# One pair of score products for both key streams of the first query tile, in a two-layer attention trunk

## The reference

```python
qr = rope(q, cos, sin)
o_slc = causal_attention(qr, rope(k_s), v_s)      # stream 0
o_win = causal_attention(qr, rope(k_w), v_w)      # stream 1
o = g[0] * o_cmp + g[1] * o_slc + g[2] * o_win
...
s = q_b @ k_b.T * scale + F[:, None] - F[None, :]
o_fox = softmax(causal(s)) @ v_b
```

## Time and profile before

| | |
|---|---|
| time, median of 3 runs | 1469.79 us (1469.35 to 1469.84) |
| the profiled execution, its own time | 1470.5 us |
| its span | 1468.7 us |
| PE busy | 1458.3 us, 99% of the span |
| DVE, ACT, POOL busy | 1033.2, 904.3, 483.8 us |
| granted clock of PE | 0.999 of full speed |

### The profile page before, as it was taken

The page is one execution under the profiler, slowest core; times in us unless marked ns, Lnnn a source line. Parts: engine busy times, 40 slices in busy tenths (PEclk is TensorE's granted clock), DMA queues, the critical chain, the costliest instruction groups (busy, mean ns, idle before and its releaser), DMA issues.

```text
span 1468.7 us, 24865 instructions
## 1 busy us (share of the span) xinstructions
PE 1458.3 (99%) x7646; PEld 1235.2 (84%) x7646; DVE 1033.2 (70%) x2405; ACT 904.3 (62%) x1889; POOL 483.8 (33%) x578
## 2 busy tenths in 40 slices
PE   9999999999999999999999999999999999999998
PEld 7888888888888888888888888888888888888887
DVE  6888877777778874444578877778788787644444
ACT  5777777777777752223466777777777777422234
POOL 1435436446445410000024446445455364000000
PEclk9999999999999999999999999999999999999999
DMA  9222222122222143332463122222112221433332
GB/s 282 64 69 59 58 58 56 46 58 58 57 58 58 45 129 100 99 101 86 108 188 80 54 57 58 57 58 59 48 55 57 57 58 48 152 88 101 100 100 90
DMA packets 213890, 117.98 MB, mean 80 GB/s; under 512 B 9304, under 2 KB 212272, under 8 KB 213296
## 3 DMA queue, kind: packets, MB, share of 16 engines
q1 hardware_dynamic: 211408, 107.49, 26.5%
q0 software_dynamic: 1728, 8.66, 1.6%
q10 hardware_dynamic: 672, 0.83, 0.2%
HBM read 110.54 MB, written 6.42 MB: 80 GB/s over the span
## 4 chain that ended last, share of the span: by engine, by line
PE 95%; ACT 2%; DMA 2%; DVE 1%; issue 0%; POOL 0%; SPq 0%; ACTq 0%; DVEq 0%; POOLq 0%
PE acc L1742 66%; PE o_pair L1822 8%; PE turned L1802 7%; PE scores L1794 4%; PE scores L1793 4%; PE misc L1833 1%; DMA w_raw<-in_w_in_dram 1%; DMA w_raw<-in_w_proj_fox_dram 1%; PE misc L1765 1%; PE o_pair L1848 1%; DMA x_nat<-in_x_dram 0%; PE turned L1937 0%; PE misc L1841 0%; ACT w_hi L751 0%; PE acc L2046 0%; PE o_pair L2046 0%
## 5 line engine op out<-in xcount | busy, mean ns | idle before, releaser
L1742 PE MATMUL acc<-u_hi,w_hi 128*128 128x512 f32 x1096 | 432.0, 394 | 0.1
L1742 PE MATMUL acc<-u_lo,w_hi 128*128 128x512 f32 x1096 | 430.7, 393 | 0.0
L1742 PE MATMUL acc<-u_hi,w_lo 128*128 128x512 f32 x1096 | 429.2, 394 | 0.0
L880 ACT ACTIVATE prob<-prob,row_max 128x128 f32<-128x128 f32 (+3 forms) x384 | 215.1, 560 | 184.0 <-DVE row_max L1331 181.7
L1155 DVE TENSOR_TENSOR w_lo<-w_raw,w_hi 128x1024 fp32r<-128x1024 f32 x184 | 230.0, 1250 | 78.9 <-ACT w_hi L751 77.3
L676 POOL TENSOR_SCALAR prob<-prob,row_inv,gates 128x128 f32<-128x128 f32 (+3 forms) x256 | 169.8, 663 | 327.6 <-DVE row_inv L1338 326.3
L751 ACT ACTIVATE w_hi<-w_raw 128x1024 fp32r<-128x1024 f32 x184 | 193.6, 1052 | 90.9 <-PE acc L1742 76.1
L1742 PEld LDWEIGHTS acc<-u_hi,w_hi 128*128 128x128 f32 x1096 | 206.0, 188 | 38.3 <-DVE w_lo L1155 0.3
L1742 PEld LDWEIGHTS acc<-u_hi,w_lo 128*128 128x128 f32 x1096 | 206.1, 188 | 37.4
L1742 PEld LDWEIGHTS acc<-u_lo,w_hi 128*128 128x128 f32 x1096 | 206.0, 188 | 36.9 <-issue 0.2
L1331 DVE CUSTOM_DVE_ANT_0 prob<-scores,causal 128x128 f32<-128x128 f32 (+3 forms) x384 | 185.0, 482 | 41.0 <-PE scores L1794 31.0
(11 more groups left out here) (253 smaller groups left out, 2290.7 us busy)
## 6 DMA issues: line engine op xcount, KB each, us to landing
w_raw<-in_w_in_dram SPq DMA_DIRECT2D x140, 512.0 KB, 3.7
w_raw<-in_w_proj_nsa_dram SPq DMA_DIRECT2D x16, 512.0 KB, 3.9
w_raw<-in_w_proj_fox_dram SPq DMA_DIRECT2D x16, 512.0 KB, 3.9
w_raw<-in_w_out_dram SPq DMA_DIRECT2D x16, 512.0 KB, 3.8
x_scratch<-xT POOLq DMA_DIRECT2D x2, 2048.0 KB, 11.0
xT<-x_scratch POOLq DMA_DIRECT2D x2, 2048.0 KB, 8.9
x_nat<-in_x_dram SPq DMA_DIRECT2D x4, 512.0 KB, 7.5
c_w<-in_cmp_w_k_dram SPq DMA_DIRECT2D x4, 512.0 KB, 6.1
```

Source lines behind the costliest of these rows:

```text
L880: act.activation(prob[:, ring, 0:width], prob[:, ring, 0:width], ACT.Exp, bias=row_max[:, ring:ring + 1], scale=-1.0, accum_out=row_sum[:, ...
L1742: ins = pe.matmul((bank or acc[par])[0:width, :], own_w, rhs, start=(n == 0), stop=(n == 23))
```

## The change

The steps of a head no longer go stream by stream. They stand in the order `NSA_ORDER`, whose entries are (stream, query tile): the first tiles of both streams come as steps 1 and 2 of the eight, and their scores are computed together, in slot 0, by one pair of products of 256 columns, into two halves of one bank of `scores`. `score_step` of step 2 then does nothing. The cost table gets the same order, with 1.0 for the joint pair and nothing for the other one. The plan that comes out for the cycles that are not a layer's last has the same 144 pieces; its units 1 and 3 end in slots 7 and 15 rather than 8 and 16, and units 2 and 4 begin in slots 7 and 15 rather than 8 and 16. The pieces in slots 0 to 11 are 70 before and 71 now, in slots 0 to 3 they are 23 both times, in slots 0 to 18 they are 116 both times. The values of the first head stand in slots 8 and 11 rather than 7 and 11, those of the second in 16 and 19 rather than 15 and 19.

```diff
+NSA_ORDER = [(0, 1), (0, 0), (1, 0), (0, 2), (0, 3), (1, 1), (1, 2), (1, 3)]
+SCORE_COST = {(0, 0): 1.0, (1, 0): 0.0}
...
+    def at(self, s):
+
+        if not self.nsa:
+            return divmod(s, QT)
+        a, qt = NSA_ORDER[s % 8]
+        return 2 * (s // 8) + a, qt
...
+    def ends(self, s):
+        return s % 8 in (4, 7) if self.nsa else s % QT == QT - 1
...
+    def score_place(self, s):
+
+        if not self.nsa:
+            return s % 2, 0
+        r = s % 8
+        return (7 * (s // 8) + (r if r < 2 else r - 1)) % 2, P if r == 2 else 0
...
                 at(plan.end[0] + 1, lambda: qk_of(0))
+                at(plan.end[0] + (4 if cycle.first or cycle.last else 3), lambda: qf_rest(parts))
                 at(plan.end[1] + 1, lambda: qk_of(1))
-                at(plan.end[0] + (4 if cycle.first or cycle.last else 3), lambda: qf_rest(parts))
...
                 def score_step(pair, s):
-                    a, qt = divmod(s, QT)
+                    a, qt = pair.at(s)
                     h, stream, branch = pair.atts()[a]
                     n, cols = key_cols(qt), slice(P * qt, P * qt + P)
-                    k_hi, k_lo = keys(pair, stream)
+                    bank, first = pair.score_place(s)
+                    if first:
+                        return
+                    both = pair.nsa and qt == 0
...
-                    to = scores[s % 2][:, 0:n]
+                    if both:
+                        to = scores[bank][:, 0:2 * P].rearrange("p (s c) -> p s c", s=2)
+                        k_hi, k_lo = kk_hi[:, pair.g, :, 0:P], kk_lo[:, pair.g, :, 0:P]
+                    else:
+                        to = scores[bank][:, 0:n]
+                        k_hi, k_lo = (k[:, 0:n] for k in keys(pair, stream))
...
-                    pe.matmul(to, q_hi, k_hi[:, 0:n], start=True, stop=False)
-                    pe.matmul(to, q_with, k_lo[:, 0:n], start=False, stop=True).then_inc(s_mm, 1)
+                    pe.matmul(to, q_hi, k_hi, start=True, stop=False)
+                    pe.matmul(to, q_with, k_lo, start=False, stop=True).then_inc(s_mm, 2 if both else 1)
```

More of the change, by code:

```diff
@@ L84, in __init__ @@
         for s in range(self.slots):
[L85 to L88, removed]
+            for lag, cost in ((-1, self.score_cost), (LAG_TURN, self.turn_cost), (LAG_PV, self.value_cost)):
+                if not last or s - lag < CYCLE_STEPS:
+                    busy[s] += cost((s - lag) % CYCLE_STEPS)
         for s, cost in ((1, 2.0), (5, 2.0), (9, 1.0), (17, 1.0)):
@@ L96, in __init__, with score_cost, turn_cost, value_cost @@
             self.end.append(next(s for s in range(self.slots) if self.cum[s] >= 24 * u + 24))
+    @staticmethod
+    def score_cost(n):
+        if n < 2 * len(NSA_ORDER) and NSA_ORDER[n % 8][1] == 0:
+            return SCORE_COST[NSA_ORDER[n % 8]]
+        return (1.0, 1.0, 1.5, 2.0)[NSA_ORDER[n % 8][1] if n < 16 else n % QT]
+    @staticmethod
+    def turn_cost(n):
+        return (0.5, 1.0, 1.5, 2.0)[NSA_ORDER[n % 8][1] if n < 16 else n % QT]
+    @staticmethod
+    def value_cost(n):
+        return 5.6 if (n % 8 in (4, 7) if n < 16 else n % QT == QT - 1) else 0.0
 class Cycle:
@@ L884, in hi_step @@
                 def hi_step(pair, s):
-                    a, qt = divmod(s, QT)
+                    a, qt = pair.at(s)
                     act.wait_ge(s_turned, pair.s0 + s + 1)
-                    if qt == 0 and not (cycle.first and pair.nsa and a < 2):
+                    if pair.starts(s) and not (cycle.first and pair.nsa and a < 2):
                         act.wait_ge(pv_mm, pair.a0 + a - 1)
@@ L1330, in max_step @@
                     apart(dve)
-                    dve.tensor_tensor_reduce(prob[:, ring, 0:width], scores[s % 2][:, 0:width],
+                    dve.tensor_tensor_reduce(prob[:, ring, 0:width], scores[bank][:, first:first + width],
                                              causal[:, T - width:T], -SCALE, BIG, ALU.add, ALU.min,
@@ L1855, in body @@
                     now = cycle.step(s - LAG_PV)
-                    if s - LAG_PV < CYCLE_STEPS and now and now[1] % QT == QT - 1:
-                        extra.setdefault(s, []).append(lambda now=now: value_step(now[0], now[1] // QT))
+                    if s - LAG_PV < CYCLE_STEPS and now and now[0].ends(now[1]):
+                        extra.setdefault(s, []).append(lambda now=now: value_step(now[0], now[0].at(now[1])[0]))
                 if cycle.first:
```

18 lines of the change are left out of this document (11 added, 7 removed).

## The result

The changed kernel takes 1478.84 us (median of four runs, 1478.55 to 1479.2) against 1469.76 us before: 9.1 us more, ratio 1.0061 with a 95% interval of 1.0049 to 1.0073. The span of the profiled execution is 1477.0 us against 1468.7.

What follows compares the result with a forecast made beforehand. PE was taken to set the pace; each cycle saves 0.43 us of work and gains 1.2 of waits, +0.8 in fourteen cycles, +11.2 on 1469.8: 1481.0 us, range 1466 to 1488.

Steps and rivals of the forecast that it cites:

- The saving: PE's score products: one pair of 128 columns less a head saves about 0.21 us, 0.43 a cycle, 6.9 in all.
- Steps A to C: ACT and DVE queues from w_hi to the low half of step 8 in a middle cycle, done at 326.76.
- Step D: First wait: PE's turn of step 10, due 326.22, waits 0.6 us (0.4 to 0.8) for step 8's low half.
- Step E: Second wait: PE's turn of step 17 waits 0.6 us (nothing to 0.8) for POOL's scaling behind the late rotation sum.
- The last cycles as even: Each layer's last cycle, with its own plan: saving and waits taken to cancel, between -0.9 and +1 us for both.
- only the first wait: Rival: only the turn of step 10 waits, 0.2 us net a cycle, 1472.6 us, up to 1475; chance 0.15.
- the signs that the prediction gave: Changed profile: PE holes before turns of steps 10 and 17, 15 us or more in the waits, cycle 58.0 us.
- No wait matters: Rival: both waits below 0.2 us, so the work saved on PE remains, 1462.9 us; chance 0.12.
- Waits and work cancel: Rival: waits of 0.43 us a cycle offset the saving, 1469.8 us, within 0.2% or 2.9 us; chance 0.08.
- The joint product saves nothing: Rival: two products of 256 columns take as long as four of 128; with both waits 1486.6 us; chance 0.05.
- step C: DVE and ACT after the reciprocal of step 7: w_lo follows at once, kf_hi starts at 321.78, kf_lo at 324.38.

Runs made afterwards that it cites:

- the best placement: The changed kernel with kf_hi, kf_lo and some weight splittings one slot later, plus output gate and v's turning, rounding, rest in last cycles: 1462.87 us, ratio 0.9954.
- the first experiment: The changed kernel with kf_hi and kf_lo one slot later in all cycles but the last of each layer: 1468.68 us, ratio 0.9994.

## Why the prediction came out as it did

**The saving: right in sum, mis-sized in its parts.** A joint pair takes 0.22 us less than two, as forecast, where PE is free to take it. The 0.43 us a cycle were measured as 0.42 (57.15 to 56.73), but only 0.29 of it are the joint products, 4.4 to 4.7 us in the whole kernel; the rest came with the new table of pieces, for which the forecast had nothing. That the sum agrees is luck. So it is in part with the 6.9 us that the best placement reached: its middle cycles have those gains and 0.12 us more from the later splitting of weights.

**Steps A to C: right to 0.15 us.** On the old clock `w_hi` starts at 308.26 (forecast 308.28), `kf_hi` at 321.92 (321.78), `kf_lo` at 324.51 (324.38), the reciprocal of step 10 at 325.93 (325.80), and the low half of step 8 is done at 326.89 (326.76). The 0.13 us come in ahead of `kf_hi`: `w_lo` took 1.43 us in this place and not 1.23, for POOL was scaling step 7 when it began.

**Step D: right in place and cause, 0.14 us short.** The wait is 0.74 us, forecast 0.6: 0.13 more for the late `kf_hi` and 0.11 more because the turn starts 0.15 us behind the low half, not 0.04; less 0.1, since the turn without a wait would start at 326.32 on the old clock (so in the first experiment), not 326.22.

**Step E: this step failed.** No wait of 0.6 us at the turn of step 17. The lateness of the rotation was right (POOL's sum starts 1.76 us later on the old clock, forecast some 1.7), but I added it to a sum of 2.26 us, a duration that belonged to its old neighbour: DVE's `w_lo` ran beside it. Started 1.76 us later, it takes 1.28. Its end is 0.8 us late, not 1.7, and the turn has 0.4 us to spare. I had called POOL's durations rough, and so had not asked why this one was twice as long as the like product beside it.

**"The last cycles as even": failed too, the other way.** They lose 1.6 us each, and the first ones 1.2 and 1.4, for which I had 0.8. I had not followed their own plans. The last cycle's loss is three waits at turns, of which that at step 5 comes of `w_lo` standing ahead of `qk_raw`, and one at `v_raw`; the first cycles have, beside the wait at step 10, one of 0.2 and 0.3 us at the turn of step 4, behind work of POOL that `w_lo` held up, and one of up to 0.5 at step 8.

So 1481.0 is nearer to 1478.8 than its parts deserve. The forecast had 14 x 0.8 = 11.2 us in first and middle cycles and nothing in the last; the trace has 3.5 in the twelve middle ones, 2.6 in the first, 3.3 in the last and -1.1 outside. Without step E and with the last cycles as even, the sum was that of the rival *only the first wait*, 1472.6 us: 6 us short. Of the signs that the prediction gave, the hole at the turn of step 10 came and the one at step 17 did not; a cycle takes 57.45 us, not 58.0; and the 19.8 us in the list of waits are above the 15 asked for only because the turns of step 8 are in it.

**The rivals.** *No wait matters* came out as a kernel of its own, 1462.87 us against 1462.9, once the extras were placed for the new plan, in part by other gains than those it counts. *Waits and work cancel* is excluded by the result, 9.1 us against its 2.9. *The joint product saves nothing* is excluded by the two kernels with two pairs.

## What to carry to other kernels

A change that takes work off the engine that sets the pace makes everything that feeds it due earlier, and a planner that then shifts its units by one slot may shift an in-order queue by one step too many. After each such change look for the turn that starts right behind another engine's work, and move the extra that stands ahead of it; here two numbers were worth 10 us, and the joint products themselves under 5.

A duration out of a trace holds for its neighbours. When one instruction takes much longer than its like, find out what ran beside it before it goes into a sum in which the neighbours move. And follow the first and last rounds of a loop by themselves when they have a plan of their own.

## What the runs showed of the hardware

POOL's elementwise instructions and DVE's `w_lo` shut each other out, whole instructions long, and the profile shows it as a longer bar, not as a wait. In the trace of the changed kernel 18 of POOL's elementwise instructions start while DVE's `w_lo` (two inputs in SBUF) is running: each is longer than its like by what was left of `w_lo`, less 0.09 to 0.16 us. In 31 more POOL starts first and `w_lo` second: POOL's take their usual time, and `w_lo` is unchanged where at most 0.11 us of POOL's work was left, 1.34 to 1.49 us long instead of 1.23 where 0.26 to 0.41 us were left, and 2.20 where 1.11 were. This is the `w_lo` of step C, timeline of POOL and of DVE:

```profile
319.88 0.77 POOL L719 TENSOR_SCALAR prob<-prob,row_inv,gates 128x512 f32<-128x512 f32 x1 [3.58 <-DVE row_inv L1382]
```

```profile
320.29 1.43 DVE L1198 TENSOR_TENSOR w_lo<-w_raw,w_hi 128x1024 fp32r<-128x1024 f32 x1
```

It is not so with every instruction of DVE. Beside the low half of a step, one of whose two inputs (`turned`) lies in the accumulator memory that PE writes, POOL's scaling of 128 columns takes its usual 0.44 us in all 14 places where over 0.6 us of the low half were left.

The experiments moved both bars both ways, the sum to 2.26 us and back, `w_lo` to 2.22 and back. The page "SBUF — State Buffer" of the Trainium skill, section "Who interferes with whom", says that a DVE instruction with two SBUF inputs contends with a GpSimd instruction that reads SBUF, and that the one issued second is blocked until the first has finished. By that rule, the trace agrees.

A product whose 256 moving columns come in two runs of 128, 512 columns apart, takes as long as one with 256 in a row. Timeline of PE in the changed kernel, a joint pair:

```profile
299.79 0.36 PE L1845 MATMUL scores<-kk_hi,q_nsa 128*128 128x256 f32 x1
...
300.33 0.40 PE L1786 MATMUL acc<-u_lo,w_hi 128*128 128x512 f32 x1
```

From the first score product to the second piece behind the pair it is 0.54 us, and 0.56 in the earlier trace rows. All pairs of 256 columns that stand between a turn and two pieces take 0.55 to 0.57 us in both traces, joint or not.
